# A decoder layer whose first stage takes features-first input, puts the contraction outside, and sends the row factor through DRAM

## The chip, the cores and the metric

The kernel runs on one core of one Trainium2 chip. The metric is the device time of one execution in microseconds. The core's engines are TensorE (PE in the profile; its weight loads are PEld), VectorE (DVE), ScalarE (ACT), GpSimd (POOL) and the sync engine (SP), which here only issues DMAs. Each engine works through its own program in order, and engines wait for each other by semaphores.

## The reference

One layer on an input x of 1024 tokens by 1024 features, float32:

```
h    = rms_norm(x, norm1_g)                     # x * rsqrt(mean(x*x) + 1e-6) * g, by token
proj = h @ w_in                                 # 1024 -> q 512 | k 512 | v 512 | xp 512 | gates 2048
q, k = rms_norm(q, q_norm_g), rms_norm(k, k_norm_g)      # 4 heads, 2 x 64 each
a    = (softmax(q1 k1^T / 8) - lam * softmax(q2 k2^T / 8)) v      # causal
a    = rms_norm(a, subln_g) * (1 - lam_init)
p    = causal_pool_mixer(xp, pool_w, pool_scale)
x    = x + (sigmoid(g0) * (a @ w_up_attn) + sigmoid(g1) * (p @ w_up_pool)) @ w_o
x    = x + square(relu(rms_norm(x, norm2_g) @ w_mlp_in)) @ w_mlp_out
```

The change touches h, the v part of proj, and how the start of the q and k part waits for them.

## The kernel before

A float32 product is made of three passes of matmuls over rounded operands: every operand is split into a high part (float32r, rounded by ScalarE) and a low part (the difference, by VectorE), and `passes` (L2297) multiplies high by high, low by high and high by low into one PSUM bank. The pair `featT` holds the normalised features, features on the partitions: 8 blocks k of 128 features by 1024 tokens. LOW and HIGH are the halves of the tokens (or of a row).

The first stage makes featT and the values v, token tile by token tile (8 tiles t of 128 tokens). SP loads the token rows of x into `x_tile` (four buffers) and the value weights into `raw`. For each tile:

- ScalarE squares the row tile and sums it (`x_square`, L1024); GpSimd makes the row factor, one column of 128 (`inverse_root`, L948, the operations at L951 and L953);
- VectorE multiplies row tile, row factor and gain into `h_row` (`x_norm`, L1507). The gain norm1_g was spread over the partitions by matmuls of a row of ones (L2506) and copied (L1207);
- TensorE transposes `h_row` in eight 128 x 128 blocks into PSUM (`x_transpose`, L2312, operation L2319); ScalarE rounds them into the high part (`x_hi`), VectorE makes the low part (`x_lo`, L1519);
- TensorE projects the tile on the 512 value columns, 24 matmuls (`v_first` for tile 0, L2496, and `v_project`, whose matmuls are at L2301), and ScalarE and VectorE split the result into `v_tok` (L1196, L1698).

The order of work is written out by hand for each engine. TensorE's is: four dummy matmuls of ones, the gain, transposes of tile 0, tile 0's matmuls mixed with the next transposes, then for each tile the transposes of the next one and its own 24 matmuls. The projection of the first query/key tile (`project(0)`, 24 matmuls with weights `slot`) stands behind value tile 5, that of the second behind value tile 6. Value tile 7 follows, then `qk_transpose(0)` (L2372) and the attention loop: `attend(0)` does three parts (nine matmuls) of the pooling projection and then the first scores (`scores`, L2422).

For a query/key tile n ScalarE squares and copies the projection (`qk_take`, L1040 and L1044), VectorE sums the squares by head (L1548), GpSimd makes the inverse roots of eight columns (L951, L953), VectorE scales the row (`qk_norm`, L1555). After the transposition ScalarE and VectorE split it into qT and kT (L1052, L1053, L1562, L1563).

Small vectors (gate bias, scales) come as 23 rows of 128 in `vec_rows`, are transposed by one matmul (L2533) and copied to `col`.

All DMAs but one (`g_one`) are issued by SP. Behind the first stage the kernel's other loads and stores follow in SP's program.

## Time and profile before

| | us |
|---|---|
| median of 3 runs | 1250.77 (1250.71 to 1251.3) |
| span of the profiled execution, first to last instruction | 1249.3 |
| TensorE busy | 1240.8 (99%) |
| VectorE busy | 937.9 (75%) |
| ScalarE busy | 556.4 (45%) |
| chain that ended last, share of TensorE | 89% |

The profile gives the execution's span; the time of an execution is what the runs list, so the median of the runs less this span, 1.5 us, is what lies around it. A row of instructions reads: start, duration of the group, engine, line of the kernel, operation, output and inputs by name, how many; in brackets the idle time of the engine before it and what ended it. A matmul's own duration (some 390 ns for 512 columns) overlaps the next one's, so the spacing of starts is the rate.

### The profile page before, as it was taken

How to read it: one execution, taken by the hardware profiler on the slowest of the kernel's cores; microseconds unless marked ns; L12 is line 12 of the kernel's file. 1: busy time of each engine (PE TensorE's matmuls, PEld its weight loads, DVE VectorE, ACT ScalarE, POOL GpSimd, SP SyncE). 2: the span in 40 equal slices, each digit the busy share in tenths (PEclk: the TensorE clock that was granted, in tenths of full speed). 3: DMA queues.
4: the chain of work that ended last, by engine and by line, in shares of the span. 5: the costliest groups of instructions: out<-in, count | busy, mean ns of one | idle time of the engine just before them, and what ended most of it. 6: DMA issues, size and time to landing. Idle time of an engine off the chain costs nothing.

```text
span 1249.3 us, 16209 instructions
## 1 busy us (share of the span) xinstructions
PE 1240.8 (99%) x5885; PEld 1022.0 (82%) x5885; DVE 937.9 (75%) x1316; ACT 556.4 (45%) x961; POOL 141.4 (11%) x198
## 2 busy tenths in 40 slices
PE   9999999999999999999999999999999999999999
PEld 6878888887788888888887888888888888888887
DVE  5547786778987778754688778778679988879764
ACT  5436665666553324322345545445445333333330
POOL 2113223223300040000000000000000000000035
PEclk9999999999999999999999999999999999999999
DMA  7100120103375457332213553453569644363223
GB/s 274 35 17 16 58 60 19 38 23 106 127 261 177 144 188 267 119 117 86 100 65 129 170 175 123 160 173 112 176 240 363 218 158 167 102 236 102 101 95 141
DMA packets 110354, 169.75 MB, mean 136 GB/s; under 512 B 5806, under 2 KB 55875, under 8 KB 110276
## 3 DMA queue, kind: packets, MB, share of 16 engines
q1 hardware_dynamic: 110274, 168.72, 39.5%
q8 instruction: 47, 0.77, 0.2%
q14 instruction: 31, 0.25, 0.1%
q10 hardware_dynamic: 2, 0.00, 0.0%
HBM read 118.37 MB, written 50.33 MB: 135 GB/s over the span
## 4 chain that ended last, share of the span: by engine, by line
PE 89%; DVE 5%; ACT 3%; issue 2%; DMA 1%; SPq 0%; POOL 0%; ACTq 0%; DVEq 0%
PE bank L2301 81%; PE bank L2443 2%; PE bank L2422 2%; PE bank L2381 1%; DVE slot_lo L1504 1%; DMA x_tile<-in_x 1%; DVE c L2201 1%; DVE pair_lo L2095 1%; PE bank L2372 1%; PE bank L2658 1%; DVE small L1587 1%; DMA gate_store<-out_tile 1%; PE bank L2319 0%; ACT slot_hi L1022 0%; ACT prob L1067 0%
## 5 line engine op out<-in xcount | busy, mean ns | idle before, releaser
L2301 PE MATMUL bank<-o_hi,s_lo 128*128 128x512 f32 (+1 forms) x452 | 175.0, 387 | 0.0
L2301 PE MATMUL bank<-o_hi,s_hi 128*128 128x512 f32 (+1 forms) x452 | 175.0, 387 | 0.0
L2201 DVE TENSOR_TENSOR c<-bank,c 128x512 f32<-128x512 f32 x112 | 75.7, 688 | 35.6 <-PE bank L2301 33.9
L2301 PE MATMUL bank<-featT_hi,pair_hi 128*128 128x512 f32 x256 | 99.9, 390 | 0.7 <-DVE c L2201 0.6
L2301 PE MATMUL bank<-o_lo,s_hi 128*128 128x512 f32 (+1 forms) x260 | 100.3, 386 | 0.0
L2301 PE MATMUL bank<-featT_lo,pair_hi 128*128 128x512 f32 x256 | 99.6, 389 | 0.0
L2301 PE MATMUL bank<-featT_hi,pair_lo 128*128 128x512 f32 x256 | 99.6, 389 | 0.0
L2301 PEld LDWEIGHTS bank<-o_hi,s_hi 128*128 128x128 f32 x452 | 84.9, 188 | 17.5
L2301 PEld LDWEIGHTS bank<-o_hi,s_lo 128*128 128x128 f32 x452 | 84.9, 188 | 17.2
L1472 ACT ACTIVATE s_hi<-s_raw 128x2048 fp32r<-128x2048 f32 x28 | 53.7, 1917 | 94.6 <-DMA s_raw<-u_store 94.6
L1448 ACT ACTIVATE c<-c 128x512 f32<-128x512 f32 x64 | 39.9, 624 | 118.8 <-DVE c L2201 118.8
L2145 DVE TENSOR_TENSOR s_lo<-s_raw,s_hi 128x2048 fp32r<-128x2048 f32 x28 | 65.7, 2345 | 22.6 <-ACT s_hi L1472 22.5
L2301 PE MATMUL bank<-slot_hi,featT_hi 128*128 128x512 f32 x192 | 78.2, 407 | 0.0
L2301 PE MATMUL bank<-slot_lo,featT_hi 128*128 128x512 f32 x192 | 75.2, 391 | 0.0
L2301 PE MATMUL bank<-slot_hi,featT_lo 128*128 128x512 f32 x192 | 74.8, 390 | 0.0
L2301 PE MATMUL bank<-comb_hi,pair_hi 128*128 128x512 f32 x192 | 74.7, 389 | 0.0
L2301 PE MATMUL bank<-comb_hi,pair_lo 128*128 128x512 f32 x192 | 74.7, 389 | 0.0
L2301 PE MATMUL bank<-o_t_lo,s_hi 128*128 128x512 f32 x192 | 74.7, 389 | 0.0
L2301 PE MATMUL bank<-comb_lo,pair_hi 128*128 128x512 f32 x192 | 74.7, 389 | 0.0
L951 POOL TENSOR_SCALAR small<-small 128x1 f32<-128x1 f32 (+1 forms) x63 | 28.7, 456 | 392.3 <-ACT h_row L1434 169.3
L1006 POOL TENSOR_TENSOR p_acc<-p_acc,shared 128x512 f32<-128x512 f32 x4 | 5.2, 1291 | 570.0 <-DVE shared L2259 570.0
L2095 DVE TENSOR_TENSOR pair_lo<-pair_f,pair_hi 128x512 fp32r<-128x512 f32 x64 | 42.8, 688 | 30.0 <-ACT pair_hi L1422 28.8
(283 smaller groups left out, 3158.0 us busy)
## 6 DMA issues: line engine op xcount, KB each, us to landing
s_raw<-u_store SPq DMA_DIRECT2D x28, 1024.0 KB, 5.6
pair_raw<-in_w_mlp_in SPq DMA_DIRECT2D x16, 1024.0 KB, 5.9
u_store<-s_tile SPq DMA_DIRECT2D x64, 256.0 KB, 2.1
o_raw<-in_w_mlp_out SPq DMA_DIRECT2D x16, 1024.0 KB, 8.3
u_store<-u_tile SPq DMA_DIRECT2D x48, 256.0 KB, 2.4
gate_store<-out_tile SPq DMA_DIRECT2D x32, 256.0 KB, 2.6
gate_raw<-in_w_in SPq DMA_DIRECT2D x8, 1024.0 KB, 5.4
raw<-in_w_in SPq DMA_DIRECT2D x12, 512.0 KB, 4.8
```

Source lines behind the costliest of these rows:

```text
L951: pool.tensor_scalar(ms, ss, 1.0 / n_mean, EPS, ALU.mult, ALU.add).then_inc(mean_sem, 1)
L1448: nc.scalar.activation(c[:], c[:], ACT.Relu).then_inc(relu_done, 1)
L1472: nc.scalar.activation(s_hi[n % 3][:], s_raw[n % 3][:], ACT.Copy).then_inc(d_hi, 1)
L1504: nc.vector.tensor_tensor(slot[1][:, 0:width], raw[r][:, 0:width], slot[0][:, 0:width], ALU.subtract).then_inc(w_ready, 1)
L1587: nc.vector.tensor_reduce(neg_max[u % 2][:, c:c + 1], score_view(u, c), AX.X, ALU.max, negate=True).then_inc(max_ready, 1)
L2095: nc.vector.tensor_tensor(pair_lo[par][:, i], src, pair_hi[par][:, i], ALU.subtract).then_inc(t_ready, 1)
L2145: nc.vector.tensor_tensor(s_lo[n % 3][:], s_raw[n % 3][:], s_hi[n % 3][:], ALU.subtract).then_inc(d_lo, 1)
L2201: nc.vector.tensor_tensor(out[:], psum, other[:], ALU.add).then_inc(up_sum, 1)
L2301: mm = nc.tensor.matmul(out, a, b, start=start and i == 0, stop=stop and i == len(steps) - 1, skip_group_check=onto)
L2372: mm = nc.tensor.transpose(bank[:, TB, i * P:(i + 1) * P], qk_row[n % 2][:, i * P:(i + 1) * P], ident[:])
L2422: mm = nc.tensor.matmul(bank[:, 2 * c + p0 // 512 if t >= 4 else 2 * j + c, 0:p1 - p0], a, b, start=i == 0, stop=i == 2)
L2443: mm = nc.tensor.matmul(*m, start=k == 0 and i == 0, stop=k == t and i == 1)
```

## The change

The program has four more inputs, laid out on the host from x, w_in and the small vectors (no arithmetic): `v_and_high[k]` has, for feature block k, 128 rows with the 512 value columns of w_in and the 512 high tokens of x transposed; `x_low[k]` the 512 low tokens transposed; `g1_cols` and `vec_cols` the gain and the small vectors as columns.

- The transposes of x, `h_row`, the spreading of the gain and the 23-row transpose are gone. featT is made from the transposed x, 512 tokens and one feature block at a time.
- The value projection is two halves of eight rounds. A round takes one feature block k for four token tiles into four PSUM banks: 12 matmuls. The high half (tiles 4 to 7) comes first and works on x times gain without the row factor; the factor is applied to the values when they leave PSUM. Then the low half (tiles 0 to 3) on fully normalised features, and project(0) and project(1) behind it.
- The row factors are made four columns at a time from the token rows, stored to DRAM by SP (`rstd_store`, 512 words), and loaded back spread over all partitions (`spread`). VectorE multiplies with it (`norm_part`), for the low half ahead of that half's rounds, for the high half (the features then replace those without the factor) beside them.
- ScalarE issues six DMAs at its start: the gain columns and the five loads of front 0 (its low half of columns), 1 and 3 and token tiles 0 and 1. The rest is issued by SP in a new order, where `spread_rstd` waits for the store.
- The splitting of value tiles 0 to 3 and the norm of query/key tiles 0 and 1 lie behind both halves; nothing lies between project(1) and qk_transpose(0).
- Semaphores are shared by more loads than before, so many waited-for counts change.

```diff
+        front = [at(f"front{k}", 128 + 4 * k, [P, D]) for k in range(KD)]
+        x_tile = [at(f"x_tile{i}", kb, [P, D]) for i, kb in enumerate((72, 80, 88, 208))]
+        spread = at("spread", 64, [P, SEQ])
...
+        V_ORDER = (4, 5, 6, 7, 0, 1, 2, 3)
...
+            def load_low(k):
+
+                sp.wait_ge(v_w_ready, k + 1)
+                sp.dma_start(front[k][:, LOW], x_low[k]).then_inc(front_in[k], 16)
...
+            def spread_rstd(half):
+
+                sp.wait_ge(x_inv, half + 1)
+                sp.dma_start(rstd_store[half].rearrange("(t p) -> p t", p=P),
+                             x_rstd[:, 4 * half:4 * half + 4], allow_slow_non_contiguous=True).then_inc(rstd_stored, 16)
+                sp.wait_ge(rstd_stored, 16 * (half + 1))
+                sp.dma_start(spread[:, HALVES[half]],
+                             rstd_store[half:half + 1].to_broadcast([P, HT])).then_inc(spread_in, 16)
...
+            sp.dma_start(front[0][:, HIGH], v_and_high[0][:, HIGH]).then_inc(high0_in, 16)
+            load_front(2)
+            load_front(4)
+            load_x(2)
+            load_x(3)
+            load_front(5)
+            load_qk(0, 0)
+            load_low(0)
+            load_front(6)
+            load_low(1)
+            load_front(7)
+            load_low(2)
+            load_qk(0, 1)
+            load_low(3)
+            spread_rstd(0)
+            for t in range(4, T):
+                load_x(t)
+            for k in range(4, KD):
+                load_low(k)
+            load_qk(0, 2)
+            load_qk(0, 3)
+            spread_rstd(1)
...
+            act.dma_start(g1_col[:], g1_cols).then_inc(vec_in, 16)
+            act.dma_start(front[0][:, LOW], v_and_high[0][:, LOW]).then_inc(front_in[0], 16)
+            act.dma_start(front[1][:], v_and_high[1]).then_inc(front_in[1], 16)
+            act.dma_start(x_tile[0][:], x_rows[0]).then_inc(x_in[0], 16)
+            act.dma_start(front[3][:], v_and_high[3]).then_inc(front_in[3], 16)
+            act.dma_start(x_tile[1][:], x_rows[1]).then_inc(x_in[1], 16)
+            for k in range(KD):
+                plain_hi_part(k)
+                v_w_hi(k)
+                if 0 < k < 5:
+                    x_square(k - 1)
+                if k == 5:
+                    qk_weights_hi(0, 0)
+            qk_weights_hi(0, 1)
+            for k in range(KD):
+                h_hi_part(0, k)
+                if k < 4:
+                    x_square(4 + k)
+                elif k < 6:
+                    qk_weights_hi(0, k - 2)
+                elif k == 6:
+                    for t in range(4, T):
+                        v_hi_part(t)
+            for k in range(KD):
+                h_hi_part(1, k)
...
+            for k in range(KD):
+                plain_lo_part(k)
+                v_w_lo(k)
+                if k == 5:
+                    qk_weights_lo(0)
+            qk_weights_lo(1)
+            norm_part(0, 0)
+            for k in range(KD):
+                if k + 1 < KD:
+                    norm_part(0, k + 1)
+                h_lo_part(0, k)
...
+            vectors()
+            for t in range(4):
+                v_lo_part(t)
+            qk_sum(0)
+            split_lo(x_w(0), 0, x_slot)
+            qk_norm(0)
+            qk_sum(1)
             qk_norm(1)
             qk_lo(0)
...
+            def v_round(half, k):
+
+                tiles = range(4, T) if half == 1 else range(4)
+                for i, (a, b) in enumerate(((0, 0), (1, 0), (0, 1))):
+                    if half == 1:
+                        pe.wait_ge((plain_hi, plain_split, v_w_ready)[i], k + 1)
+                        if i == 0:
+                            pe.wait_ge(v_w_rounded, k + 1)
+                    elif i < 2:
+                        pe.wait_ge((h_hi, h_split)[i], k + 1)
+                    for t in tiles:
+                        mm = nc.tensor.matmul(bank[:, v_bank(t), :], featT[a][:, k, columns(t)], v_w[b][:, k, :],
+                                              start=k == 0 and i == 0, stop=k == KD - 1 and i == 2)
+                        if k == KD - 1 and i == 2:
+                            mm.then_inc(v_full, 1)
...
+            for i in range(8):
+                nc.tensor.matmul(bank[:, v_bank(0), :], ones[:, 0:P].bitcast(F32R), ones[:].bitcast(F32R), start=True, stop=True)
+            for half in (1, 0):
+                for k in range(KD):
+                    v_round(half, k)
+            for n in range(2):
+                for k in range(KD):
+                    project(n, k)
             qk_transpose(0)
```

## Rows read from the trace of the kernel before

**Rows 1.** Busy sums by stretch: window, its length, each engine, granted clock, DMA.

```profile
0.00:76.32 76.32, 74.38 (x326) 57.61 (x326) 41.23 (x71) 35.91 (x61) 14.39 (x30) 1.00 0.40 133
76.32:1249.30 1172.98, 1166.41 (x5559) 964.39 (x5559) 896.62 (x1245) 520.45 (x900) 126.96 (x168) 1.00 0.40 136
```

**Rows 2.** Timeline of TensorE: start us, us, line, operation, count.

```profile
7.17 1.94 PE L2319 MATMUL bank<-ident,h_row 128*128 128x128 f32 x8
...
11.82 1.68 PE L2496 MATMUL bank<-v_w_hi,featT_lo 128*128 128x512 f32 x4
...
15.87 0.70 PE L2496 MATMUL bank<-v_w_hi,featT_hi 128*128 128x512 f32 x2
...
31.37 1.09 PE L2319 MATMUL bank<-ident,h_row 128*128 128x128 f32 x8
...
73.42 0.60 PE L2372 MATMUL bank<-ident,qk_row 128*128 128x128 f32 x4
...
76.32 0.33 PE L2422 MATMUL bank<-kT_hi,qT_hi 64*128 64x128 f32 x2 [0.23 <-DVE kT_lo L1563]
```

**Rows 3.** The chain that ended last: start us, us, what.

```profile
57.24 16.36 PE bank L2301 x72
```

**Rows 4.** Timeline of ScalarE at its start.

```profile
1.26 1.28 ACT L1200 ACT_TABLE_LOAD   x1 [1.26 <-PEq L2749]
3.24 0.63 ACT L1200 ACTIVATE square<-x_tile 128x512 f32<-128x512 f32 x1 [0.69 <-DMA x_tile<-in_x]
...
4.38 0.63 ACT L1202 ACTIVATE square<-x_tile 128x512 f32<-128x512 f32 x1 [0.42 <-DMA x_tile<-in_x]
...
6.88 1.06 ACT L1191 ACTIVATE v_w_hi<-raw 128x1024 fp32r<-128x1024 f32 x1 [1.77 <-DMA raw<-in_w_in]
...
11.41 1.06 ACT L1027 ACTIVATE square<-x_tile 128x1024 f32<-128x1024 f32 x1 [0.55 <-DMA x_tile<-in_x]
```

**Rows 5.** Busy sums of two short stretches; the last two numbers are DMA share, GB/s.

```profile
5.00:10.00 5.00, 4.92 (x13) 2.39 (x12) 3.32 (x4) 2.87 (x6) 0.87 (x2) 1.00 1.00 353
...
15.00:20.00 5.00, 5.00 (x28) 4.21 (x26) 3.87 (x5) 3.27 (x6) 1.82 (x4) 1.00 1.04 368
```

**Rows 6.** DMAs: issue durations (ns, min/median/max), and size and us to landing.

```profile
L592 SPq DMA_DIRECT2D raw<-in_w_in x4: 427/469/706, 1.6 to 3.7; - x4
...
attn_store<-attn_kept SPq DMA_DIRECT2D x16, 128.0 KB, 2.1
...
x_tile<-in_x SPq DMA_DIRECT2D x2, 256.0 KB, 2.8
```

**Rows 7.** ScalarE's groups by line, 0 to 74 us: busy us, mean ns, idle before.

```profile
L1033 ACT ACTIVATE featT_hi<-bank 128x512 fp32r<-128x512 f32 x16 | 8.7, 595 | 1.4 <-PE bank L2319 1.3
L1027 ACT ACTIVATE square<-x_tile 128x1024 f32<-128x1024 f32 x7 | 7.5, 1064 | 0.6 <-DMA x_tile<-in_x 0.5
...
L1027 ACT ACTIVATION_READ_ACCUMULATOR square<-x_tile 128x1 f32 x7 | 1.4, 198 | 0.0
```

**Rows 8.** VectorE's groups by line, 0 to 76.3 us.

```profile
L1519 DVE TENSOR_TENSOR featT_lo<-bank,featT_hi 128x512 fp32r<-128x512 f32 x16 | 10.4, 684 | 1.5 <-ACT featT_hi L1033 1.3
...
L1686 DVE SCALAR_TENSOR_TENSOR h_row<-x_tile,small,bank 128x512 f32<-128x512 f32 x2 | 1.5, 748 | 5.1 <-POOL small L986 5.0
```

**Rows 9.** Timeline around the norm of query/key tile 1 and the first split.

```profile
68.17 0.60 ACT L1040 ACTIVATE qk_square<-bank 128x512 f32<-128x512 f32 x1 [4.84 <-PE bank L2301]
...
68.80 0.69 DVE L1548 TENSOR_REDUCE small<-qk_square 128x8 f32<-128x512 f32 x1 [4.15 <-ACT qk_square L1040]
...
69.86 1.64 POOL L953 TENSOR_TENSOR small<-small 128x8 f32<-128x8 f32 x1
...
75.46 0.42 DVE L1562 TENSOR_TENSOR qT_lo<-bank,qT_hi 128x256 fp32r<-128x256 f32 x1
75.79 0.47 DVE L1563 SCALAR_TENSOR_TENSOR kT_lo<-bank,small,kT_hi 128x256 fp32r<-128x256 f32 x1
```

**Rows 10.** DMA packets in the window 36 to 40 us.

```profile
DMA packets 1951, 0.98 MB, mean 246 GB/s; under 512 B 32, under 2 KB 1951, under 8 KB 1951
```

More of the change, by code:

```diff
@@ new lines, in v_hi_part @@
+                if t == 0:
+                    act.wait_ge(h_ready, 2 * KD)
+                if t < 4:
+                    nc.scalar.activation(v_tok[:, :, t, 0, :], k4(bank[:, v_bank(t), :], HEADS), ACT.Copy).then_inc(v_hi, 1)
+                else:
+                    act.wait_ge(x_inv, 2)
+                    nc.scalar.activation(v_tok[:, :, t, 0, :], k4(bank[:, v_bank(t), :], HEADS), ACT.Copy,
+                                         scale=x_rstd[:, t:t + 1]).then_inc(v_hi, 1)
+            act.dma_start(g1_col[:], g1_cols).then_inc(vec_in, 16)
@@ new lines, in _ @@
+            qk_weights_hi(0, 1)
[10 more added lines that the diff above has]
+                h_hi_part(1, k)
+            act.wait_ge(lam_step, 2)
+            nc.scalar.activation(lam_exp, lam_sum, ACT.Exp).then_inc(lam_exped, 1)
@@ L2501, in _ @@
-            pe.wait_ge(zeroed, 1)
-            for i in range(4):
-                nc.tensor.matmul(bank[:, v_bank(1), :], ones[:, 0:P].bitcast(F32R), ones[:].bitcast(F32R), start=True, stop=True)
-            pe.wait_ge(g_in, 16)
-            for i, half in enumerate((LOW, HIGH)):
-                nc.tensor.matmul(bank[:, (TB, OUT)[i], :], ones[0:1, 0:P], g_one[:, half], start=True,
-                                 stop=True).then_inc(vec_full, 1)
-            pe.wait_ge(const_ready, 1)
-            x_transpose(0)
@@ L2754 @@
         args.append(nc.dram_tensor(f"in_{name}", a.shape, mybir.dt.from_np(a.dtype), kind="ExternalInput").ap())
+    columns = np.asarray(inputs["x"]).reshape(1024, 8, 128).transpose(1, 2, 0)
+    v_rows = np.asarray(inputs["w_in"]).reshape(8, 128, -1)[:, :, 1024:1536]
+    vectors = [np.asarray(inputs["b_gate"]).reshape(-1), np.asarray(inputs["pool_scale"]).reshape(-1),
+               np.asarray(inputs["subln_g"]).reshape(-1)]
+    for name in ("q_norm_g", "k_norm_g"):
+        vectors.append(np.tile(np.asarray(inputs[name]).reshape(-1), 2))
+    laid_out = {
+        "v_and_high": np.concatenate([v_rows, columns[:, :, 512:]], axis=2),
+        "x_low": columns[:, :, :512],
+        "g1_cols": np.asarray(inputs["norm1_g"]).reshape(8, 128).T,
+        "vec_cols": np.concatenate(vectors).reshape(-1, 128).T,
+    }
+    for name, a in laid_out.items():
+        a = np.ascontiguousarray(a)
+        arrays[f"in_{name}"] = a
+        args.append(nc.dram_tensor(f"in_{name}", a.shape, mybir.dt.from_np(a.dtype), kind="ExternalInput").ap())
     args.append(nc.dram_tensor("out_y", inputs["x"].shape, F32, kind="ExternalOutput").ap())
```

358 lines of the change are left out of this document (120 added, 238 removed).

## The prediction

> **What bounds the kernel now.** Read the busy sums by stretch first [rows 1]. TensorE is busy 74.38 of the first 76.32 us and 1166.41 of the 1172.98 us behind them, so the end of the program follows TensorE, and whatever the first stage gains or loses is carried to the end almost whole. The change ends where the first scores begin, so the quantity to forecast is the start of that matmul, 76.32 us now [rows 2].
>
> Next the order of TensorE's work in the stage. The dense part runs at 0.227 us a matmul (72 in 16.36 us, [rows 3]). The value projection is 8 tiles of 24 matmuls, the first two query/key tiles are 48 more: 240 x 0.227 = 54.5 us. The features are turned by 64 transposes, eight to a tile, 1.09 us for eight where they run dense [rows 2]: 8.7 us. Transposes start at 7.17 and the stage's last block (the turning of query/key tile 0) at 73.42, which is 66.25 us; 54.5 + 8.7 = 63.2 leaves 3 us of slow start and small waits. Part of that is the clock: four matmuls at 11.82 took 1.68 us (0.42 each, the rate of the 1.2 GHz level), two at 15.87 took 0.70, as at 2.4 GHz, although the granted clock reads 1.00 all along [rows 1, 2]. Between 73.42 and the scores TensorE has nine matmuls of filling and one gap of 0.23 us.
>
> So TensorE has hardly a hole now. The change takes work out of it, and asks the transfers and the row factor to keep up with a shorter stage. They decide.
>
> **The transfers.** ScalarE's first instructions show landings: 0.26 MB by 3.24, 0.52 by 4.38, 1.05 by 6.88 and 2.62 by 11.41 us [rows 4], which is 0.30 MB/us from 4.4 to 11.4 us. Later windows move 0.353 and 0.368 MB/us [rows 5], with the engines' share at 1.00 and over: the limit is reached. I take 0.36 from 11.4 on. Before its first half of rounds can end the new stage needs 4.19 MB of fronts (eight of 512 KB, weights beside the high half of x), 2.10 MB of token rows 0 to 3 for the squares; 1.05 MB of query/key weights and 1.05 MB of low halves lie in the same queue ahead of the factor's store: 8.39 MB together.
>
> **Start.** ScalarE issues six DMAs before its first activation, five more than now; one issue is about 0.47 us [rows 6], so the last goes out near 3.7 and the table load of 1.28 us [rows 4] ends near 5.0. High part 0 and value weight 0 are rounded by 6.1 (0.54 us each, 8.7 / 16, [rows 7]). The first value matmul comes at 6.1, before the first transpose of now (7.17). The eight dummies are 4 x 0.52 x 2 = 4.2 us from 1.3 on (2.08 us for four now), under this wait: they cost nothing.
>
> **First half (tiles 4 to 7, eight rounds of 12 matmuls, 2.73 us each).** If nothing is late it runs from 6.1 to 27.9. Five loads are in ScalarE's queue, and both queues are full from 4 us on. No row shows two at once. I let them share evenly; if ScalarE's went first its 2.36 MB would be in by 10.6 and this half would not stall. Then front 1 (total 1.57 MB) lands at 7.9, x 0 and front 4 (2.62) at 11.4, front 3 and x 2 (3.67) at 14.3, x 1 and x 3 (4.72) at 17.2. The scalar program is in order: round 1, square 0, round 2, square 1, round 3. A square is 1.06 + 0.2 - 0.1 = 1.16 us [rows 7]. So: round 1 rounded at 9.0; square 0 waits for 11.4, ends 12.6; round 2 at 13.7; square 1 waits for 17.2, ends 18.4; round 3 at 19.5; square 2 20.6, round 4 21.7, square 3 22.9. TensorE starts round 3 at 19.5 where it wanted 14.3, and five rounds later stands at 33.1: 5.2 us of stall, most of it the wait for token tile 1. The later fronts (18.7, 22.3, 24.5 for 5, 6, 7) are in time. VectorE has per round a product 0.75 and a difference 0.65 us [rows 8], 1.4 against 2.73, hidden; if it were not, each 0.1 us over would cost 0.8.
>
> A rule of the Trainium skill speaks against the second queue. The trace shows only one queue at work, at share 1.00 [rows 5]. The page DMA: Bandwidth & Descriptors, section Queues, rings and completion order, says that each DMA engine goes round robin over the queues it has work for, packet by packet; its section Issuing engines are not separate DMA queues adds that issuing from several engines saves only the sequencer's time. By it front 3 and x 1 wait as above; served in order of issue all of 4.72 MB is still ahead of x 1, so the sum moves little.
>
> **The row factor, first trip.** Squares end 22.9. GpSimd's two operations took 69.49 to 71.50, 2.0 us, for eight columns [rows 9]; for four this is the upper end. 24.9. The store stands behind 8.39 MB in SP's ring: 11.4 + 5.77 / 0.36 = 27.4. No row shows a store of 512 words of 4 bytes. Lower bound: an empty-queue store of 128 KB lands in 2.1 us [rows 6], the issue counted; behind a draining ring some 1 us of that is left. For the packets, 1951 short ones went through in a window of 4 us [rows 10], 512 would be 1.05. Upper bound by the same row: four times that per packet, 4.2 us more. I take 28.4. The spread back (256 KB) is like the load of 256 KB from an empty queue, 2.8 us [rows 6]: 31.3 with the issue. Product 0.75 and rounding 0.6: TensorE could go on at 32.7. So the second half starts at 33.1, with both limits within half a microsecond: removing either alone gives little, so the share of the two queues hardly matters. The same DMA page, section Specifications, says that below 512 bytes the engine does read-modify-write; no run here shows it, and by it the store would be nearer the upper bound and the sum 3 us longer.
>
> **Second half and what runs beside it.** Eight rounds: 33.1 to 54.9. SP issues x 4 to 7 only behind the first trip, so they land from 32.8 to 37.2, low halves 4 to 7 by 40.1, the last query/key weights by 43.1. Squares 4 to 7 sit between ScalarE's roundings of the half: rounding 4 is done at 39.6, wanted at 44.0; rounding 7 at 47.4, wanted 52.2. Hidden. The second trip ends near 47 (squares 39.1, factor 41, store behind the ring 44.1, spread 47). Then VectorE has eight times 1.35 us, vectors 1.5, values of tiles 0 to 3 and the sum of tile 0: the norm of query/key tile 0 comes at about 66.5. TensorE, after 48 x 0.227 = 10.9, asks for it at 65.8. These 0.7 us are within my error; I count half. Query/key block at 66.2 instead of 73.42: 7.2 us earlier.
>
> **The wait that replaces one.** Now value tile 7 lies between query/key tile 1 and the scores, and the norm of tile 1 (3.33 us from the square at 68.17 to the inverse root's end at 71.50, [rows 9]) runs under it. After the change nothing does, and the VectorE order puts norm 1 ahead of the splitting of query tile 0, which the scores need. From the end of the projection: 3.33 for the chain to the inverse root, 0.65 for the norm (as the differences, [rows 8]), 0.33 + 0.47 for the two splits, 0.04: 4.8. With the projection's end at 66.1 to 66.3 scores start at 71.1. TensorE's filling covers 2.5, so some 2.3 us are idle, 2.1 more than now. Removed otherwise and not counted again: the gain row copies, the 23-row transpose (0.24 us).
>
> **Sum.** 76.32 - 71.1 = 5.2 us earlier. The span is 1249.3, and 1.5 lie around it by the median of 1250.77. 1249.3 - 5.2 = 1244.1 span, 1245.6 by the clock of the runs.
>
> **Rivals.**
> (A) The forecast, 0.50: 1243.5 to 1247.
> (B) Transfers keep up, 0.20. For it: the ring moved more than 0.36 where rows were wide, and fronts and x rows are all 4 KB wide. At 0.40 MB/us from 2 us on the 8.39 MB are in by 23, the trip ends near 28.5, the second half starts at 30.3: 2.8 less, 1242.8. Were TensorE never to wait, 6.1 + 54.5 + 5.1 = 65.7 against 76.32: 1240.2; against it, the store cannot pass the ring.
> (C) The slow clock comes back after the waits, or the tiny store is at its upper bound, 0.20. The waits ahead of rounds 2 and 3 are 2 to 3 us each. Twelve us into the stage the kernel still runs at 1.2 GHz [rows 2]; each 4 us at that level hold half the work, 2 us lost for each. One or two, or 3 us of the store: 1247.6 to 1249.6. Against it: round 0 and 1 at half rate would be free, they wait anyway.
> (D) Slower than before, 0.10. One mechanism: the round trip of the factor through DRAM. TensorE has nothing to do in it, and it is paid in front of the second half. It decides from where the second half starts later than 38.6 (33.1 + 5.2 + 0.3), so from a trip of over 12 us from the last square's factor to the spread instead of 6.4. If ring and packets take 14, the second trip slips too (VectorE has no slack there) and TensorE stands 3 us more: 1254. For it: the trip was never made before, SP is blocked for it and holds back x 4 to 7. Against it: stores in the kernel land in 2.1 us.
> That the change does nothing is not possible on the path: 8.7 us of transposes leave TensorE. All of them given back is between (C) and (D).
>
> **Chances.** About 0.2% (2.5 us) is what a measurement can tell from no change. Faster: all of A and B, two fifths of C: 0.78. Same 0.12, slower 0.10. Range 1242.3 to 1249.3: B's good end and C's bad one, some 0.2 left out.
>
> **What would show it.** Right: no ident<-h_row rows; the value matmuls run k outside, from about 6 us; a wait of TensorE ahead of round 3 that ends on ScalarE behind a square that waited for DMA; a second wait, or none, at 31 to 34 us on VectorE's product behind the spread; 1 to 3 us idle ahead of the first scores. The rest of the span unchanged in length. Wrong: a start of the second half before 30 or after 37, matmuls of 0.43 us behind a wait, or a gap of TensorE behind 76 us that is not there now.

## The result, and the profile after

The changed kernel is slower. Its median is 1260.15 us (1260.09 to 1260.86, 4 runs) against 1250.74 (1250.31 to 1251.3, 4 runs) of the kernel before beside it: ratio 1.0074, 95% interval 1.006 to 1.0089. The span is 1259.1 us against 1249.3, 9.8 more.

Busy sums by stretch of the changed kernel, columns as in [rows 1], with more windows behind (engines in the order PE, PEld, DVE, ACT, POOL, then granted clock, DMA share, GB/s):

```profile
0.00:39.55 39.55, 26.34 (x104) 20.19 (x104) 14.90 (x36) 17.58 (x29) 2.82 (x12) 0.94 0.70 250
39.55:85.27 45.72, 40.53 (x158) 32.45 (x159) 32.55 (x53) 23.12 (x41) 6.62 (x6) 0.87 0.34 109
85.27:1259.10 1173.83, 1166.60 (x5560) 965.17 (x5559) 896.64 (x1245) 520.53 (x900) 126.39 (x168) 1.00 0.40 136
...
35.00:40.00 5.00, 0.45 (x1) 0.45 (x2) 1.81 (x3) 1.13 (x2) 0.00 (x0) 0.50 1.00 310
40.00:45.00 5.00, 5.00 (x13) 3.84 (x13) 4.02 (x7) 5.00 (x10) 0.00 (x0) 0.50 1.02 392
45.00:50.00 5.00, 5.00 (x23) 4.07 (x22) 2.94 (x5) 3.17 (x6) 2.08 (x2) 0.97 0.57 169
```

Read the third row first. Behind the first scores the program takes 1173.83 us against 1172.98 [rows 1]: 0.85 of the 9.8. The other 8.95 lie ahead of 85.27, where 76.32 stood before. TensorE is busy for 26.34 + 40.53 = 66.87 us there instead of 74.38, so the transposes did go, and still the stage is longer: 18.4 us of it are idle, 1.9 before.

TensorE's timeline shows where. Start, length, operation, count, and in brackets the idle time before it and what ended it:

```profile
6.52 1.17 PE L2516 MATMUL bank<-v_w_hi,featT_hi 128*128 128x512 f32 x4 [1.72 <-ACT v_w_hi L1063]
...
18.42 1.16 PE L2516 MATMUL bank<-v_w_hi,featT_hi 128*128 128x512 f32 x4 [1.91 <-ACT v_w_hi L1063]
...
39.55 2.07 PE L2516 MATMUL bank<-v_w_hi,featT_hi 128*128 128x512 f32 x4 [7.28 <-ACT featT_hi L1070]
...
80.38 1.11 PE L2399 MATMUL bank<-ident,qk_row 128*128 128x128 f32 x4 [5.19 <-DVE qk_row L1594]
...
85.27 0.47 PE L2450 MATMUL bank<-kT_hi,qT_hi 64*128 64x128 f32 x2
```

Two waits stand out, 7.28 us ahead of the second half and 5.19 ahead of the turning of query/key tile 0 (73.42 before, [rows 2]). Behind the first, four matmuls take 2.07 us instead of 1.07 to 1.17. The windows above give the granted clock for that: 0.50, the 1.2 GHz level, from 35 to 45 us.

What stands behind both waits is in the chain of waits (start, length, what):

```profile
3.19 12.78 DMA x_tile<-in_x
...
21.86 1.05 POOL small L976
...
22.93 10.41 DMA rstd_store<-small
...
33.36 4.70 DMA spread<-rstd_store
...
38.09 0.76 DVE front L1554
...
47.50 8.33 DMA rstd_store<-small
...
55.85 5.70 DMA spread<-rstd_store
...
61.57 0.76 DVE front L1554
...
73.66 2.48 DVE v_tok L1730 x4
...
77.11 2.50 POOL small L976
...
79.64 0.70 DVE qk_row L1594
...
80.38 1.11 PE bank L2399 x4
```

A store of 2 KB takes 10.41 us, the second one 8.33, and each holds up a transfer, of 4.70 and 5.70 us. That is 29.1 us for the two round trips. Everything from 61.57 to 80.38 is one unbroken chain of VectorE, with a little of ScalarE and GpSimd.

The store's packets are not what takes so long. The packet counts of 23.7 to 24.3 us and of 24.3 to 33 us:

```profile
DMA packets 528, 0.00 MB, mean 4 GB/s; under 512 B 528, under 2 KB 528, under 8 KB 528
```

```profile
DMA packets 1, 0.02 MB, mean 2 GB/s; under 512 B 0, under 2 KB 0, under 8 KB 0
```

The last loads pass until 23.6 us, the store's packets, all under 512 bytes, from 23.8 to 24.2; up to 33 us the trace then has one packet, on another queue. The semaphore comes at 33.34, nine microseconds after the last packet of the store. The second store, issued at 47.50, finds the last loads draining until 48.3, its packets pass from 48.4 to 48.8, and it waits until 55.83 all the same.

### The profile page after: what moved, and what is told of

Same layout as the page of the kernel before. It is cut to its first block, busy times and chain, and to the rows that moved or that the text cites. A ratio compares the mean times of both kernels' runs of the same rounds, so it can differ in the third digit from the quotient of the medians.

```text
span 1259.1 us, 16093 instructions
## 1 busy us (share of the span) xinstructions
PE 1233.5 (98%) x5820; PEld 1017.8 (81%) x5820; DVE 944.1 (75%) x1334; ACT 561.2 (45%) x969; POOL 135.8 (11%) x186
## 4 chain that ended last, share of the span: by engine, by line
PE 84%; DVE 7%; DMA 3%; ACT 3%; issue 2%; POOL 0%; ACTq 0%; DVEq 0%
PE bank L2341 77%; PE bank L2471 2%; PE bank L2450 2%; DMA rstd_store<-small 1%; PE bank L2408 1%; DMA x_tile<-in_x 1%; DMA spread<-rstd_store 1%; PE bank L2399 1%; DVE c L2241 1%; ACT x_tile L1049 1%; DVE pair_lo L2135 1%; DVE slot_lo L1536 1%; PE bank L2650 1%; DVE small L1626 1%; POOL small L976 0%
## 5 line engine op out<-in xcount | busy, mean ns | idle before, releaser
L2341 PEld LDWEIGHTS bank<-o_hi,s_hi 128*128 128x128 f32 x452 | 84.9, 188 | 17.2
L974 POOL TENSOR_SCALAR small<-small 128x1 f32<-128x1 f32 (+2 forms) x58 | 25.8, 444 | 410.5 <-ACT h_row L1466 169.3
```

Of the source, the lines that this page charges most:

```text
L974: pool.tensor_scalar(ms, ss, 1.0 / n_mean, EPS, ALU.mult, ALU.add).then_inc(mean_sem, 1)
L2341: mm = nc.tensor.matmul(out, a, b, start=start and i == 0, stop=stop and i == len(steps) - 1, skip_group_check=onto)
```

## The experiments

The theory was that the landing of the 512 words of 4 bytes is the whole loss, and the first question was what makes it slow. The rivals: the number of writes, the draining ring, the clock behind the wait, the second queue. Each ratio is to the kernel before, run beside it. In experiments 2, 4, 5 and 6 the row factor is left out of the features, in experiment 1 it is there but stands at the wrong tokens; those kernels serve to time the store, and only the others compute the layer.

**1. 128 runs of 16 bytes instead of 512 of 4.** The factors come back in another order than the tokens.

```
-  sp.dma_start(rstd_store[half].rearrange("(t p) -> p t", p=P),
+  sp.dma_start(rstd_store[half].rearrange("(p t) -> p t", t=4),
```

> The changed kernel with the factor stored in the order of the partitions, 128 runs of 16 bytes instead of 512 of 4 (the spread factors then stand in another order). Theory (the store's 10.4 and 8.3 us come from the number of tiny writes): landing falls to 4 us or less, each trip is 5 to 6 us shorter, scores near 75, time 1250. Rival (the store is slow because of its place behind a full queue, or any store to DRAM that is read back is): landing stays at 8 us or more, time 1260.

Measured: 1248.96 us (1247.14 to 1249.82, 10 runs), ratio 0.9978 [0.9969, 0.9988]; span 1247.6. SyncE's own timeline of it; since SP waits for the store ahead of the spread, the time between the two is the store's landing (1.47 and 2.02 us):

```profile
23.42 0.34 SPq L612 DMA_DIRECT2D rstd_store<-small  x1
24.89 0.33 SPq L615 DMA_DIRECT2D spread<-rstd_store  x1
...
40.14 0.34 SPq L612 DMA_DIRECT2D rstd_store<-small  x1
42.16 0.34 SPq L615 DMA_DIRECT2D spread<-rstd_store  x1
```

and TensorE's:

```profile
18.92 1.80 PE L2516 MATMUL bank<-v_w_hi,featT_hi 128*128 128x512 f32 x4 [2.15 <-ACT v_w_hi L1063]
...
34.21 1.07 PE L2516 MATMUL bank<-v_w_hi,featT_hi 128*128 128x512 f32 x4
...
68.60 0.66 PE L2399 MATMUL bank<-ident,qk_row 128*128 128x128 f32 x4 [1.60 <-DVE qk_row L1594]
...
72.66 0.33 PE L2450 MATMUL bank<-kT_hi,qT_hi 64*128 64x128 f32 x2 [1.32 <-DVE kT_lo L1602]
```

The second half starts at 34.21 without a wait. It could have started at about 32: in this execution round 3 ran at the slow clock behind its wait of 2.15 us (granted clock 0.74 from 20 to 25 us) and took 4.4 us instead of 2.8, and the block, which still waits 1.60 us for VectorE, hides that. The scores come 12.6 us earlier than in the changed kernel and the time is now below that of the kernel before. So the loss was in the store. It doesn't say yet whether the number of writes or their places were at fault.

**2. The same 512 words, each 512 bytes from the next.** The spread reads the gain row instead of the factor, since the words no longer lie in one row.

```
-  rstd_store = nc.dram_tensor("rstd_store", [2, HT], F32, kind="Internal").ap()
+  rstd_store = nc.dram_tensor("rstd_store", [2, HT, P], F32, kind="Internal").ap()
...
-  sp.dma_start(rstd_store[half].rearrange("(t p) -> p t", p=P),
+  sp.dma_start(rstd_store[half, :, 0].rearrange("(t p) -> p t", p=P),
...
-               rstd_store[half:half + 1].to_broadcast([P, HT])).then_inc(spread_in, 16)
+               norm1_g[:, HALVES[half]].to_broadcast([P, HT])).then_inc(spread_in, 16)
```

> The changed kernel with each of the 512 words of the factor stored 512 bytes from the next, and the spread loaded from a row of norm1_g behind the wait for that store. Theory (number of tiny writes): the landing stays at 8 to 10 us. Rival (the writes hinder each other because they fall into the same 2 KB of DRAM): the landing falls to about 3 us. The spread load then reads bytes that nobody has just written: if it lands in 2.8 instead of 4.7 us, reading just written bytes costs the difference.

Measured: 1247.28 us (1246.68 to 1248.78, 8 runs), ratio 0.9971 [0.996, 0.9981]. SyncE's timeline:

```profile
23.27 0.37 SPq L612 DMA_DIRECT2D rstd_store<-small  x1
25.10 0.34 SPq L615 DMA_DIRECT2D spread<-in_norm_g  x1
...
39.16 0.37 SPq L612 DMA_DIRECT2D rstd_store<-small  x1
41.36 0.34 SPq L615 DMA_DIRECT2D spread<-in_norm_g  x1
```

The same number of writes of the same size lands in 1.83 and, the second time, 2.20 us. So the number of writes alone costs nothing. Nor does nearness alone: the 128 runs of experiment 1 lie side by side in the same 2 KB and land as fast. It takes many writes that are neighbours.

**3. TensorE kept busy in the two waits**, to see what the clock is worth: 32 matmuls of filling ahead of the second half and 20 ahead of the block.

```
...
+  for k in range(KD):
+      v_round(1, k)
+  fill_wait(0, 32)
+  for k in range(KD):
+      v_round(0, k)
...
+  pe.wait_ge(v_ready, 4)
+  fill_wait(6, 20)
```

> The changed kernel with 32 more dummy matmuls between the two halves of rounds and 20 ahead of the block of query/key tile 0, where TensorE stood for 7.3 and 5.3 us. Theory (the fall of the clock is a consequence that costs only where TensorE is the last): the granted clock stays 1.00, the rounds of the second half take 21.8 instead of 24.6 us, but the block of tile 0 still waits for VectorE behind the second trip and starts at 80.4; only the slow matmuls behind it are gained, 2 to 2.5 us, time 1258. Rival (the slow stretches are simply added): 5 us gained, 1255.

Measured: 1261.39 us (1259.62 to 1262.26, 4 runs), ratio 1.008 [1.0065, 1.0095]. TensorE's timeline and its windows:

```profile
40.41 1.20 PE L2516 MATMUL bank<-v_w_hi,featT_hi 128*128 128x512 f32 x4 [0.25 <-ACT featT_hi L1070]
...
81.15 1.12 PE L2399 MATMUL bank<-ident,qk_row 128*128 128x128 f32 x4 [3.27 <-DVE qk_row L1594]
...
86.04 0.47 PE L2450 MATMUL bank<-kT_hi,qT_hi 64*128 64x128 f32 x2
```

```profile
75.00:80.00 5.00, 2.88 (x13) 2.06 (x11) 3.72 (x6) 3.68 (x7) 2.33 (x2) 1.00 0.01 2
80.00:85.00 5.00, 3.85 (x11) 3.24 (x12) 2.55 (x5) 0.75 (x2) 2.21 (x3) 0.53 0.32 103
```

The second half ran at full clock, 21.9 us instead of 24.6, and the block came no sooner (81.15 against 80.38): what the clock gave went into the wait for VectorE. So the slow clock of 35 to 45 us is a consequence off the path, not a part of the loss. The filling ended too early for the last wait, the clock fell again behind it, and the 1258 us that the theory gave were missed. That second slow stretch is on the path: from block to scores the changed kernel takes 4.89 us, experiment 1 takes 4.06.

**4. No trip at all.** The factor is not stored, nothing waits for it; the gain row is spread in its place, the first time at once and the second behind the first product.

```
-  sp.wait_ge(x_inv, half + 1)
-  sp.dma_start(rstd_store[half] ... ).then_inc(rstd_stored, 16)
-  sp.wait_ge(rstd_stored, 16 * (half + 1))
+  if half == 1:
+      sp.wait_ge(h_ready, 1)
...
-               rstd_store[half:half + 1].to_broadcast([P, HT])).then_inc(spread_in, 16)
+               norm1_g[:, HALVES[half]].to_broadcast([P, HT])).then_inc(spread_in, 16)
```

> The changed kernel without the trip of the row factor: no wait for the factor and no store of it; the spread comes from a row of norm1_g at the same place in SP's program (the features are not scaled by the row factor; all instructions of the engines remain). Theory (the store's landing of 8 to 10 us was the loss, the rest of the trip of 6 us is hidden behind the first half of rounds): little better than the store with 128 runs, the second half of rounds starts at 31.5 as there, scores at 71.5 to 72.5 instead of 72.7, time 1247.5 to 1248.5. Rival (the whole trip through DRAM is on the path, short or long): the scores come 4 us or more earlier than with 128 runs, time 1245.

Measured: 1246.61 us (1244.87 to 1248.38, 5 runs), ratio 0.9963 [0.995, 0.9976]; span 1243.1. TensorE's timeline and its windows:

```profile
64.77 0.60 PE L2397 MATMUL bank<-ident,qk_row 128*128 128x128 f32 x4
...
69.80 0.33 PE L2448 MATMUL bank<-kT_hi,qT_hi 64*128 64x128 f32 x2 [2.35 <-DVE kT_lo L1600]
```

```profile
65.00:70.00 5.00, 2.65 (x17) 1.91 (x15) 2.11 (x4) 1.69 (x4) 1.84 (x2) 1.00 0.13 45
70.00:75.00 5.00, 5.00 (x33) 4.22 (x32) 1.66 (x6) 1.02 (x5) 0.00 (x0) 1.00 0.00 0
```

The scores come at 69.80, 2.86 us ahead of experiment 1 and 1.86 ahead of experiment 2 (71.66), where the theory said 0.2 to 1.2 and the rival 4 or more: a short trip costs 2 to 3 us. By the ratios it is 1 to 2 us, and beside experiment 2 that is within the noise. What it costs is seen in the chains of waits. Here TensorE has no wait from 18.43 us to the block, at 64.77; its second half starts at 32.12 (the 31.5 that the expectation gives for experiment 1 is the start of round 7 there, the second half started at 34.21). In experiment 1 the block waits for VectorE, whose chain goes back to a load that SP issued behind the first trip:

```profile
30.66 9.97 DMA raw<-in_w_in
```

Against the changed kernel (85.27) the two trips with all that follows them cost 15.5 us.

**5 and 6. The same words at four more distances**: 32 and 64 bytes in one kernel, 8 and 16 in the next (first and second store). The spread reads the gain row.

```
...
+  words_apart = [rstd_store[0].rearrange("n c -> (n c)").rearrange("(n c) -> n c", c=8)[0:HT, 0], rstd_store[1, :, 0]]
-  sp.dma_start(rstd_store[half].rearrange("(t p) -> p t", p=P),
+  sp.dma_start(words_apart[half].rearrange("(t p) -> p t", p=P),
```

> As with the words of the factor 512 bytes apart, but 32 bytes apart in the first store and 64 in the second (the spread comes from a row of norm1_g). Theory (words of one short piece of DRAM, written by different DMA engines, wait for each other; with 4-byte steps 8 or 16 words share one): both land in 2 to 3 us, the first a little later if a piece is longer than 32 bytes. Rival (it is the whole 2 KB to 4 KB region or a page that they share): 16 KB and 32 KB are still few pages, landings of 5 us and more.

> The words of the factor 8 bytes apart in the first store and 16 in the second (the spread comes from a row of norm1_g). Theory (words that share a short piece of DRAM, of 32 bytes or so, and come from different DMA engines, wait for each other, so the landing falls with their number in a piece): 8 bytes apart 5 to 6 us, 16 bytes apart 3 to 4 us. Rival (only directly neighbouring words hinder each other): both land in 2 to 2.5 us.

Measured, one run each: 1247.27 and 1248.45 us. SyncE's timeline of the kernel with 8 and 16 bytes, landing read as in experiment 1:

```profile
23.12 0.37 SPq L614 DMA_DIRECT2D rstd_store<-small  x1
27.36 0.34 SPq L617 DMA_DIRECT2D spread<-in_norm_g  x1
40.53 0.37 SPq L614 DMA_DIRECT2D rstd_store<-small  x1
43.33 0.34 SPq L617 DMA_DIRECT2D spread<-in_norm_g  x1
```

| us from issue to landing, by distance of the words in bytes | 4 | 8 | 16 | 32 | 64 | 512 | runs of 16 B, no gap |
|---|---|---|---|---|---|---|---|
| first store | 10.41 | 4.24 | - | 1.98 | - | 1.83 | 1.47 |
| second store | 8.33 | - | 2.80 | - | 2.18 | 2.20 | 2.02 |

In every one of these stores the packets are through 1.1 to 1.7 us after the issue. What is left until the landing is 9.1 and 7.0 us at 4 bytes, 2.9 at 8, 1.1 at 16 (where loads still passed beside it), and 0.4 to 0.7 in all others. So the wait is nearly gone where two words share 32 bytes, and gone where each has them alone. Each distance but 4 and 512 bytes was stored once, and the stretch of DRAM grows with the distance, so the two are not told apart.

**7. The factor turned before it is stored.** VectorE turns 32 x 32 blocks of it, four DMAs store runs of 128 bytes in token order.

```
+  nc.vector.transpose(factor[:], small[:, 28 + 4 * half:60 + 4 * half]).then_inc(turned, 1)
...
+  for b in range(4):
+      sp.dma_start(rstd_store[half].rearrange("(t b i) -> b t i", b=4, i=32)[b],
+                   factor[32 * b:32 * b + 4, :]).then_inc(rstd_stored, 16)
```

> The changed kernel with the factor turned by VectorE in blocks of 32 x 32 first and stored in token order by four DMAs of four runs of 128 bytes each, all else as it is. Theory (only the way the words fall into DRAM matters): the four land in 2.5 us, one issue of 0.35 us each in front; second half of rounds at 31.5 to 32, scores at 73, time 1249. Rival (the 11 us gained with 128 runs of 16 bytes have to do with something else in that kernel): landing above 6 us, time above 1255.

Measured: 1252.15 us (1251.56 to 1253.46, 10 runs), ratio 1.0012 [1.0002, 1.0021]. A miss. The landing is short (27.81 to 30.00, 2.2 us), but VectorE, whose program is in order, reaches the turning late: the store is issued at 27.81 instead of 23.4. The turning stands behind the low parts of the last round in VectorE's program and runs at 27.58. The second half starts at 36.22 behind 3.66 us of waiting.

**8. The same with the small vectors computed early** (in the second half, not behind it) and 8 + 6 matmuls of filling ahead of block and scores.

```
+  if k == 4:
+      vectors()
...
+  fill_wait(3, 8)
+  qk_transpose(0)
...
+  fill_wait(3, 6)
+  scores(0)
```

> As the kernel with turned factors, and besides: the small vectors are loaded and worked on inside the second half of rounds, where VectorE waits for data anyway, and 8 dummy matmuls stand ahead of the block of query/key tile 0, 6 ahead of the first scores. Theory (what is left over against the forecast is VectorE's chain, 1.5 us of it small vectors, and a slow clock behind TensorE's waits of 1.6 and 1.3 us): the block starts 1.5 us earlier, the granted clock stays at 1.00 from 70 to 80 us, scores to second scores take 7.7 instead of 9.2 us, time 1246. Rival (the clock falls for another reason, or the dummies delay real work): 1248 or more.

Measured: 1251.95 us (1250.82 to 1252.89, 10 runs), ratio 1.0008 [0.9998, 1.0017]. The block moves from 72.30 to 71.35 and the scores from 76.36 to 75.41, 1 us, and the granted clock stays at 1.00 from 70 to 80 us, as the theory had it; in the time neither shows.

**9. Runs of 16 bytes, and VectorE puts them in order**: its products read the spread factor at a step of 4 words.

```
-  now = front[k][:, HALVES[half]]
-  nc.vector.scalar_tensor_tensor(now, now, g1_col[:, k:k + 1], spread[:, HALVES[half]],
+  now = k4(front[k][:, HALVES[half]], 4)
+  turned = spread[:, HALVES[half]].rearrange("q (p t) -> q t p", t=4)
+  nc.vector.scalar_tensor_tensor(now, now, g1_col[:, k:k + 1], turned,
```

> The factor stored as 128 runs of 16 bytes as before, and VectorE reads the spread with a step of four words, so that every token has its own factor: the change as it was meant, with one access pattern turned on each side. Theory (the way the words fall into DRAM is the whole difference between slower and faster): as with 128 runs, landing 1.5 to 2 us, scores at 72.7, time 1247 to 1249.5, faster than before. Rival (VectorE reads every fourth word more slowly): the eight products of the second half take more than 0.75 us each, the norm of tile 0 comes later, time 1251 or more.

Measured: 1251.65 us (1251.3 to 1252.31, 11 runs), ratio 1.0007 [0.9998, 1.0016]. The group of the products, of experiment 1 and of this one (busy us, mean ns, idle before):

```profile
L1554 DVE SCALAR_TENSOR_TENSOR front<-front,g_col,spread 128x512 f32<-128x512 f32 x16 | 11.8, 746 | 1.7 <-DMA spread<-rstd_store 1.1 <-DMA front<-in_x_low 0.6
```

```profile
L1555 DVE SCALAR_TENSOR_TENSOR front<-front,g_col,spread 128x512 f32<-128x512 f32 x16 | 17.9, 1129 | 1.8 <-DMA spread<-rstd_store 1.0 <-DMA front<-in_x_low 0.8
```

and TensorE's timeline:

```profile
71.80 1.11 PE L2400 MATMUL bank<-ident,qk_row 128*128 128x128 f32 x4 [6.71 <-DVE qk_row L1595]
```

The rival was right: a product takes 1129 ns where it took 746, and since VectorE's chain sets the block, the block is 3.2 us later. The second half starts in time, at 32.29, and it helps nothing.

**10. With early vectors and filling on top.** The edits of 8 on 9.

> The same with the small vectors inside the second half of rounds, and dummies (8 ahead of the block of query/key tile 0, 6 ahead of the first scores). Theory (what is left is VectorE's chain and the slow clock behind two waits): block at 67.5, scores at 71.5 to 72, clock 1.00 behind them, time 1246 to 1247. Rival: no gain over the kernel without them, the waits only move.

Measured: 1251.64 us (1249.59 to 1252.59, 10 runs), ratio 1.0005 [0.9996, 1.0014]. The block comes at 70.66, 1.1 us earlier, but the scores at 77.16: the filling itself ran at a granted clock of 0.50 from 70 to 75 us and stood in their way.

**11. All loads from one queue.** Experiment 9 with the five loads of ScalarE's queue issued by SP, in the same order.

```
-  act.dma_start(front[1][:], v_and_high[1]).then_inc(front_in[1], 16)
...
+  load_front(2)
+  load_front(1)
+  load_front(4)
+  load_x(0)
```

> As with the strided factor, but the five loads of ScalarE's queue issued by SP, in the order in which the two queues issue them: that part of the change undone. Theory (both queues share the transfers evenly, and the DMA engines are the limit): token tile 1 lands where it does now, within 1 us, round 3 starts at 18.5; nothing else moves, time within 1 us of the strided kernel. Rival 1 (the second queue gives a head start): every early load lands 1 to 2 us later, time 1 to 2 us longer. Rival 2 (the second queue holds the early loads back): front 1 and token tiles 0 and 1 land earlier, first half of rounds shorter by 2 us.

Measured: 1252.07 us (1250.55 to 1253.14, 10 runs), ratio 1.0007 [0.9997, 1.0017], against 1251.65 of experiment 9. TensorE's waits for value weights sum to 4.6 us instead of 3.7, and the first store lands in 2.65 us. The medians differ by 0.4 us, less than the noise. The second half starts 1.65 us later (33.94 against 32.29), mostly by the clock in round 3, but the block waits for VectorE in both, so this kernel doesn't show what the second queue would be worth where TensorE is the path.

**12. Experiment 10 with x 1 and x 2 exchanged and the first spread issued by ScalarE.**

```
-  act.dma_start(x_tile[1][:], x_rows[1]).then_inc(x_in[1], 16)
+  act.dma_start(x_tile[2][:], x_rows[2]).then_inc(x_in[2], 16)
...
+  act.wait_ge(rstd_stored, 16)
+  act.dma_start(spread[:, LOW], rstd_store[0:1].to_broadcast([P, HT])).then_inc(spread_in, 16)
```

> As the kernel with early vectors and dummies, and besides: token tiles 1 and 2 change places between the queues, and the first spread is issued by ScalarE, so that SP issues the loads behind the store without waiting for it. Theory (without the trip the ring never runs dry, which was worth 3 us of scores): tile 1 lands by 11 us, the first half of rounds ends at 29.5 to 30.5, second half at 31, VectorE's idle time in it goes, scores at 69.5 to 70.5, time 1244 to 1245. Rival (the second half is held by what VectorE and ScalarE do, not by the transfers): 1246 or more.

Measured: 1251.96 us (1250.4 to 1252.94, 11 runs), ratio 1.0006 [0.9997, 1.0015]. Round 3 no longer waits (1.89 us in experiment 9) and starts at 17.75. The spread takes 6.1 us, so the second half waits 1.56 us and starts at 33.07, and the block still waits 3.5 us for VectorE, at 71.42. So bringing the loads forward doesn't shorten this kernel.

**13. ScalarE puts the factor in order**, one copy per half; VectorE reads it straight.

```
...
+  act.wait_ge(spread_in, 16 * (half + 1))
+  nc.scalar.activation(k4(spread[:, HALVES[half]], 4), spread_raw[half].rearrange("q (p t) -> q t p", t=4),
+                       ACT.Copy).then_inc(spread_turned, 1)
...
-  dve.wait_ge(spread_in, 16 * (half + 1))
+  dve.wait_ge(spread_turned, half + 1)
```

> Factor stored as 128 runs of 16 bytes and brought into token order by one more copy of ScalarE for each half, with VectorE reading it without a step. Theory (the store and VectorE's chain are all that decides): products of VectorE back at 0.75 us, one copy of 0.6 to 0.9 us in each trip, second half of rounds at 32.2, scores 73 to 73.5, time 1248.5 to 1250. Rival (token order is not to be had without the loss): above 1251.

Measured: 1247.88 us (1247.46 to 1249.82, 8 runs), ratio 0.9979 [0.9968, 0.9989]; span 1246.0. TensorE's timeline:

```profile
68.35 0.66 PE L2409 MATMUL bank<-ident,qk_row 128*128 128x128 f32 x4 [3.02 <-DVE qk_row L1604]
...
72.57 0.33 PE L2460 MATMUL bank<-kT_hi,qT_hi 64*128 64x128 f32 x2
```

The second half starts at 32.39. This kernel leaves nothing of the work out, and it is 3.2 us (ratio 0.9979) faster than the kernel before: that is what the change is worth with its store mended.

**14. The version that the experiments point to.** On 13: low halves and tiles 4 to 7 loaded in turn, small vectors early, x 1 and x 2 exchanged, and query tile 0 split ahead of the norm of tile 1.

```
   for k in range(4, KD):
       load_low(k)
+      load_x(k)
...
   qk_sum(1)
+  qk_lo(0)
   qk_norm(1)
-  qk_lo(0)
```

> The same, and besides: low halves and token tiles 4 to 7 loaded in turn, the small vectors inside the second half of rounds, token tiles 1 and 2 changed between the queues, and query tile 0 split before the norm of tile 1. Theory (VectorE's chain is the path up to the block of tile 0, and its order the path from there to the scores): the block starts within 0.5 us of the projection's end at 66.5 to 67, the scores 2.5 to 3 us behind it without a wait, at 70, time 1244.5 to 1246. Rival (the transfers set the pace of the second half): TensorE waits inside it, scores at 72 or later, time 1248 or more.

Measured: 1247.2 us (1246.51 to 1249.32, 9 runs), ratio 0.9972 [0.9962, 0.9981]. TensorE's timeline:

```profile
32.40 1.19 PE L2528 MATMUL bank<-v_w_hi,featT_hi 128*128 128x512 f32 x4 [0.70 <-ACT featT_hi L1078]
...
69.12 1.11 PE L2411 MATMUL bank<-ident,qk_row 128*128 128x128 f32 x4 [3.79 <-DVE qk_row L1605]
...
74.00 0.44 PE L2462 MATMUL bank<-kT_hi,qT_hi 64*128 64x128 f32 x2
```

It beats the kernel before; from experiment 13 it can't be told apart. The 1244.5 to 1246 that I expected are missed: round 3 no longer waits and starts at 17.94, and the scores no longer wait, but the block waits 3.79 us for VectorE, whose chain, with a little of ScalarE and GpSimd's 2.5 us in it, runs almost without a hole from 49.9 us to 69.1. The first store, issued at 20.98 behind loads that pass until 23.7, lands in 3.4 us: that is what a draining ring costs it.

## Why the prediction was wrong

I forecast 1245.6 us in a range of 1242.3 to 1249.3 and gave "slower" 0.10; it is 1260.15. The terms of the sum up to 23 us held, but for the rate of the loads. One term in the middle was wrong by an order of magnitude.

**What held.** The first value matmul came at 6.52 (6.1 forecast), front 1 at 8.5 (7.9), x 0 at 11.1 (11.4). Token tile 1 was the late one, as argued, and landed at 16.0 (17.2), so TensorE began round 3 at 18.42 (19.5), and the first half ended at 32.3 (33.1). GpSimd's two operations took 1.24 us for four columns and was done at 22.9 (24.9). The two queues moved 54% and 47% of the engines' time from 4 to 8 us: they share evenly. From the block to the scores it took 4.89 us (4.9), and that is luck: no idle in it, and matmuls at the 1.2 GHz level, where the forecast had full clock and 2.3 us idle.

**The rate of the loads** was taken too low: 0.36 MB/us, where the windows from 5 to 15 us show 0.41 to 0.42. The 8.39 MB were in by 23.6 us, not by 27.4, as rival B had it. By itself it moves little, since by the forecast the first half ended at 33.1 anyway.

**The step that failed** is "The row factor, first trip", in the sentence "Upper bound by the same row: four times that per packet, 4.2 us more. I take 28.4." The landing was put 1.0 us behind the end of the loads; it came 9.7 us behind it. The price was built from two things, an empty-queue store and a count of packets [rows 6, 10], and neither has in it what decides. The packets passed faster than I took, in half a microsecond. The store landed at 33.34 all the same, 10.41 us after its issue. Experiment 2 shows that 512 writes of 4 bytes are no burden by themselves (1.83 us), and experiments 5 and 6 that with them the landing follows how close the words lie. My upper bound assumed that the cost goes with the number of packets, so it couldn't hold the value. Of the 1951 packets of [rows 10] only 32 are under 512 bytes; no row of before has words of different partitions side by side in DRAM, and "no row shows it" should have meant a range open upward, on a step that the whole second half hangs on.

The Trainium skill, page DMA: Bandwidth & Descriptors, section Specifications, says that below 512 bytes the engine does read-modify-write; by it I would have come near the upper bound, 3 us more. The measurement decides against it as a price per write: words of 4 bytes that lie 32 bytes apart or more land in 2 us. Its section Anatomy of one DMA, on transfers that GpSimd issues, puts most of a transfer's fixed 2 us on the receipt of the last byte written. This store is issued by SP; its trace agrees in the place of the time, behind the last packet, not in its size, 9 us here.

**The spread** was priced at 2.8 us plus issue as a plain load of 256 KB [rows 6]; it took 4.70 and 5.70. From the gain row, which nothing had just written, it took 3.2 to 5.0 us in experiments 2, 5 and 6, from a row just written 3.2 (experiment 7, second trip) to 5.3 in the kernels with a short store (6.1 where ScalarE issued it). Experiments 1 and 2 issue it at nearly the same times and differ by 0.4 and 0.6 us (5.2 and 3.9 from the fresh row, 4.8 and 3.3 from the gain row). So most of the excess doesn't come from the row's being fresh; how it divides between the spreading and the traffic beside it was not told apart.

**The second trip.** Forecast: spread at 47. Measured 61.55, which is 14.5 later: 6.5 because the squares of tiles 4 to 7 sit between the roundings of a half that started late (factor at 47.5, not 41), 5.2 in the store (8.33 against 3.1 behind the ring) and 2.8 in the spread. I had written that VectorE has no slack there; so the block came at 80.38 instead of 66.2, 14.2 later, nearly the same number. The clock's 2.8 us in the second half lie beside that chain and cost nothing, as experiment 3 shows; the stretch at the slow clock behind the block adds some 0.8.

**Rival D** named the mechanism and its point: the second half later than 38.6 means slower than before. It started at 39.55. Its price, 1254, was too low. Already by its own terms, 2 us past the point where the gain is gone and 3 more, it comes to 1255.8, and it let the second trip slip by too little for the wait of 5.2 us ahead of the block. It had 0.10 because "stores in the kernel land in 2.1 us" stood against it, a row of stores with whole rows in them.

**The rest of the idea was sound.** With the store alone mended the second half starts at 32.4 to 34.2 (experiments 13 and 1), and time and span of experiment 1 come out at 1248.96 and 1247.6 us, inside the range. The 3.4 us over my number are 1.6 us until the scores (72.66 against 71.1), about 1.5 in the tile behind them, where the granted clock was 0.88 and 0.78 behind two short waits, and what separates one run from the next. Of the other suspects, the second queue makes no difference clear of the noise (experiment 11), and the clock is not on the path while VectorE is (experiment 3).

**Still open.** Why neighbouring words hinder each other is not shown, only that they do and how it falls with distance. The Trainium skill, page Collectives: The Full Stack, section Rules for kernel authors, says that buffers aligned to 32 bytes prevent the hardware's read-modify-write; that most of the cost is gone at 32 bytes fits such a piece, but no run here tells it from another mechanism. The 128 runs of 16 bytes share such pieces by twos as well, and land in 1.5 to 2.0 us, so sharing alone is not enough. Whether the words' coming through different DMA engines matters wasn't tried.

## What to carry to other kernels

Price a small store by its landing, not by its bytes or packets: if anything waits for it, look for a row with the same pattern in DRAM, and if there is none, leave the range open upward and measure it alone first. When single words of many partitions go to DRAM, let each partition write a run (16 bytes were enough here) and put the order right on an engine with slack; the engine that reads with a step pays for it, so it must not be the one on the path. And a round trip that blocks an in-order queue costs its own time plus whatever that queue would have issued: here 2 to 3 us up to the scores for two trips whose stores landed in 1.5 and 2.0.

## What the runs showed of the hardware

- 512 words of 4 bytes, side by side in DRAM and from 128 partitions, land 10.41 and 8.33 us after their issue (10.8 and 8.6 in experiment 3), though their packets are through within 1.3; at 8, 16 and 32 bytes of distance it is 4.24, 2.80 and 1.98 us.
- A row of 2 KB spread to 128 partitions (256 KB) lands in 3.2 to 5.7 us, and once in 6.1 from ScalarE's queue, a plain load of 256 KB in 2.8 [rows 6].
- A VectorE product of 128x512 with one operand at a step of 16 bytes takes 1129 ns instead of 746. The Trainium skill, page SBUF — State Buffer, section Door 1: The DMA port swizzle, tells of lines of 16 bytes in which neighbouring reads run at full rate; the trace agrees, each read here falls in a new line and the product takes 1.5 times as long.
- The granted clock stood at 0.50 for about 10 us around the wait of 7.3 us (35 to 45), and again at 0.50 from 80 to 85 us behind one of 5.2 us. Behind the waits of 1.3 to 4.0 us near 70 us it was between 0.50 and 1.00 from kernel to kernel. Runs of one kernel then differ by up to 3.5 us (1244.87 to 1248.38 in experiment 4) where the changed kernel's four lie within 0.8. The clock goes with it: in experiments 2, 4 and 14 the runs with a mean granted clock of 0.997 took 1247.81 to 1249.32 us and all others 1244.87 to 1247.48. In experiment 1 two of ten runs don't fit, so that the clock is the reason is likely, not shown.
